# First-wave token lists of two mixture-of-experts layers: added up on the chip instead of read back from DRAM

## The chip, the cores and the metric

One core of a Trainium2 chip runs the whole program. The metric is the device time of one execution in microseconds (us), the median of several runs. Lower is better.

## The reference

Two decoder layers on 1024 tokens of width 1024. Each layer has a mixer and then a mixture of experts; both layers' mixtures have this form:

```python
grp_p, grp_idx = lax.top_k(softmax(xf @ wg_group + bg_group), 1)              # 1 of 4 groups
top_p, top_local = lax.top_k(softmax(in_grp), 2)                              # 2 of its 8 experts
expert_id = grp_idx * EXPERTS_PER_GROUP + top_local
gate = grp_p * top_p / jnp.sum(top_p, axis=-1, keepdims=True)
...
return (jax.nn.silu(xb @ w_gate[e]) * (xb @ w_up[e])) @ w_down[e]             # 1024 -> 256 -> 1024
...
y = jnp.zeros_like(x_tok).at[tok_sorted].add(y_buf[dest] * gate_sorted[:, None])
```

There are 32 experts and 2048 (token, expert) pairs, so an expert gets 64 rows in the mean. Everything is float32.

## The kernel before

The program is a row of blocks. Between two blocks all engines meet: GpSimd (POOL) collects an arrival from each of them and releases them. At some of these places POOL also clears semaphores, with a second meeting behind that; one such place is between the two blocks of this case in the second layer, and none in the first. The blocks of this case occur once in each layer: `project_and_route` (names that begin with `out_`) and `experts` (`ex_`). Rows of the first layer say `even`, those of the second `odd`.

**`project_and_route`** goes through 8 tiles of 128 tokens. In a tile TensorE multiplies by the mixer's output matrix (L1004, each operand split into a high and a low part, so three products stand for one), turns the result (L1025), and multiplies by the router's weights (L1033). VectorE adds the residual (`add_residual`, L871), norms (`norm`, L878), picks the group (`choose_group`, L897 to L905) and the two experts (`choose_experts`, L912 to L922), and finds out where the tile's pairs stand in their experts' lists (`place`, L927 to L935). For that, `count` on TensorE (L1040) multiplies the one-hot choices `both` by a triangle of ones, which gives the number of earlier tokens with the same expert. POOL then writes each pair's token number and result slot into a DRAM table, at row rank * 32 + expert, with two indirect DMAs per tile (L794). The order of work is written out by hand: PE's loop, DVE's loop and POOL's loop each name their steps tile by tile.

After the last tile POOL waits until all 16 table writes have landed, reads the first 128 ranks of all lists back (`Lists.load`, L655), waits for that too, and issues the gathers of the first two experts' rows (`Lists.gather`, L659). VectorE works out the gates and then the low parts of the first expert's weights, which have been loaded in three pieces (two for gate and up, one for down; L987). ScalarE makes the high parts (L852).

**`experts`** works through 32 experts in waves of at most 128 rows each; in this data's executions the first wave is the one that the profile shows. `start` brings up expert 0 and part of expert 1, and `step` then runs once per expert. `turn_x` on TensorE (L1274) turns the gathered rows, ScalarE and VectorE split them (`tokens`, L1348 and L1414), `gate_up` (L1285) makes 12 products for each of the pieces FIRST and SECOND, `gate` and `product` give the hidden values (L1353, L1421), `turn_h` turns them (L1294), and `down` makes 12 products (L1306). Weights of later experts stream in on SP's queue into four buffers, three of which are filled by `project_and_route`; each weight piece is split by ScalarE (`high`, L1338) and VectorE (`low`, L1405) before it is used.

The order at the start of `experts`, and the waits that POOL has at its beginning:

```python
def start(n):            # TensorE
    turn_x(n, 0)
    gate_up(n, 0, FIRST)
    gate_up(n, 0, SECOND)
    turn_x(n, 1)
...
pool.wait_ge(listed, 16 * 2 * NT)
lists.load(pool, 0)
...
def begin():             # POOL, in experts
    pool.wait_ge(zeroed, 1)
    for e in range(2, B):
        gather(0, e)
```

## Time and profile before

| what | us |
|---|---|
| three runs | 2034.01, 2034.46, 2036.6 |
| their median | 2034.46 |
| span of the profiled execution, first to last instruction | 2024.6 |
| what lies around the span (median less span) | 9.9 |
| TensorE busy | 1792.8 (89% of the span) |
| VectorE, ScalarE, POOL busy | 1199.3, 882.3, 312.6 |

The profiled execution's own device time is not listed apart from the three runs; its span is, and the three runs lie within 0.13% of each other. In the profile PE is TensorE's matmuls, PEld its weight loads, DVE VectorE, ACT ScalarE, SP the queue that issues most loads. PEclk is the clock granted to TensorE: 1.00 is 2.4 GHz and 0.50 is 1.2 GHz. A float32 product is shown as two instructions, a product of split (fp32r) or bf16 operands as one. The two places of this case are short against the span: about 31 us in the first layer (846 to 877) and 30 us in the second (1630 to 1660).

### The profile page before, as it was taken

How to read it: one execution, taken by the hardware profiler on the slowest of the kernel's cores; microseconds unless marked ns; L12 is line 12 of the kernel's file. 1: busy time of each engine (PE TensorE's matmuls, PEld its weight loads, DVE VectorE, ACT ScalarE, POOL GpSimd, SP SyncE). 2: the span in 40 equal slices, each digit the busy share in tenths (PEclk: the TensorE clock that was granted, in tenths of full speed). 3: DMA queues.
4: the chain of work that ended last, by engine and by line, in shares of the span. 5: the costliest groups of instructions: out<-in, count | busy, mean ns of one | idle time of the engine just before them, and what ended most of it. 6: DMA issues, size and time to landing. Idle time of an engine off the chain costs nothing. (4 is left out here: it accounts for less than half of the span.)

```text
span 2024.6 us, 25845 instructions
## 1 busy us (share of the span) xinstructions
PE 1792.8 (89%) x9691; PEld 1486.2 (73%) x9691; DVE 1199.3 (59%) x1551; ACT 882.3 (44%) x1060; POOL 312.6 (15%) x254
## 2 busy tenths in 40 slices
PE   8999999577999999759999965999999949999990
PEld 7888889475788888647888744888878837888770
DVE  4323433556655445659999858333235558999884
ACT  4102222362333332338888844111112128888870
POOL 0000000001000001123443310000000123344320
PEclk8999999777999999979999986999999969999995
DMA  5433332802000043559999958111206368999976
GB/s 200 144 120 120 112 130 70 169 1 84 1 1 1 1 153 138 187 220 367 381 373 374 373 205 272 42 52 41 93 4 223 115 243 335 385 381 372 371 282 258
DMA packets 145011, 374.26 MB, mean 185 GB/s; under 512 B 39918, under 2 KB 74862, under 8 KB 120158
## 3 DMA queue, kind: packets, MB, share of 16 engines
q1 hardware_dynamic: 113254, 309.38, 41.6%
q0 software_dynamic: 22432, 45.53, 6.3%
q10 hardware_dynamic: 9216, 17.93, 2.3%
q8 instruction: 64, 1.05, 0.2%
q14 instruction: 45, 0.37, 0.1%
HBM read 331.21 MB, written 75.10 MB: 201 GB/s over the span
## 5 line engine op out<-in xcount | busy, mean ns | idle before, releaser
L1285 PE MATMUL ex_ps_h<-even_split 128*128 128x512 f32 x768 | 194.7, 404 | 7.9 <-DVE even_split L1414 7.6
L1285 PE MATMUL ex_ps_h<-odd_split 128*128 128x512 f32 x768 | 193.1, 402 | 8.0 <-DVE odd_split L1414 7.8
L1285 PEld LDWEIGHTS ex_ps_h<-even_split 128*128 128x128 f32 x768 | 141.7, 191 | 46.8 <-DVE even_split L1414 14.2
L1285 PEld LDWEIGHTS ex_ps_h<-odd_split 128*128 128x128 f32 x768 | 140.3, 189 | 46.8 <-DVE odd_split L1414 14.4
L520 PE MATMUL in_ps<-in_w_hi,in_xT_hi 128*128 128x512 f32 (+1 forms) x448 | 172.5, 385 | 1.7 <-DVE in_xT_lo L425 1.7
L520 PE MATMUL in_ps<-in_w_lo,in_xT_hi 128*128 128x512 f32 (+1 forms) x448 | 169.2, 378 | 0.0
L520 PE MATMUL in_ps<-in_w_hi,in_xT_lo 128*128 128x512 f32 (+1 forms) x448 | 169.2, 378 | 0.0
L1689 PE MATMUL conv_ps<-conv_xT_hi,conv_w_hi 128*128 128x512 f32 x384 | 150.2, 391 | 0.9 <-DVE conv_w_lo L1627 0.9
L1689 PE MATMUL conv_ps<-conv_xT_lo,conv_w_hi 128*128 128x512 f32 x384 | 149.7, 390 | 0.0
L1689 PE MATMUL conv_ps<-conv_xT_hi,conv_w_lo 128*128 128x512 f32 x384 | 149.6, 390 | 0.0
L2410 ACT ACTIVATE att_prob<-att_ps_s 128x512 f32<-128x512 f32 x114 | 67.9, 597 | 154.0 <-PE att_ps_s L2345 153.9
L432 DVE COPY in_stage<-in_ps 128x512 f32<-128x512 f32 (+1 forms) x56 | 36.7, 656 | 161.7 <-PE in_ps L520 161.7
L2359 PE MATMUL att_ps_o<-mix_v,att_prob 128*128 128x128 f32 x912 | 121.4, 278 | 0.4 <-DVE even_attended L2472 0.4
L2359 PEld LDWEIGHTS att_ps_o<-mix_v,att_prob 128*128 128x128 f32 x912 | 117.8, 194 | 4.4 <-ACT att_prob L2410 0.8
L2438 DVE TENSOR_REDUCE att_low<-att_ps_m 128x2 f32<-128x768 f32 (+7 forms) x80 | 71.7, 914 | 49.2 <-PE att_ps_m L2310 47.1
L520 PEld LDWEIGHTS in_ps<-in_w_hi,in_xT_hi 128*128 128x128 f32 x448 | 84.8, 189 | 17.8 <-DVE in_xT_lo L425 2.1
L520 PEld LDWEIGHTS in_ps<-in_w_hi,in_xT_lo 128*128 128x128 f32 x448 | 84.7, 189 | 15.5
L520 PEld LDWEIGHTS in_ps<-in_w_lo,in_xT_hi 128*128 128x128 f32 x448 | 84.9, 190 | 14.4
L1689 PEld LDWEIGHTS conv_ps<-conv_xT_hi,conv_w_hi 128*128 128x128 f32 x384 | 72.4, 188 | 16.1 <-DVE conv_w_lo L1627 1.3
L1004 PE MATMUL out_ps_o<-even_split,even_x_hi 128*128 128x512 f32 x256 | 81.6, 400 | 2.5 <-DVE even_x_lo L939 2.5
L1689 PEld LDWEIGHTS conv_ps<-conv_xT_hi,conv_w_lo 128*128 128x128 f32 x384 | 72.2, 188 | 15.2
L1306 PE MATMUL ex_ps_y<-odd_split,ex_h_hi 128*128 128x512 f32 x256 | 81.8, 401 | 1.6 <-DVE ex_h_lo L1428 1.6
(342 smaller groups left out, 3965.0 us busy)
## 6 DMA issues: line engine op xcount, KB each, us to landing
all_region<-in_moe_w_gate SPq DMA_DIRECT2D x16, 1024.0 KB
all_region<-in_moe_w_up SPq DMA_DIRECT2D x16, 1024.0 KB
all_region<-in_moe_w_down SPq DMA_DIRECT2D x16, 1024.0 KB
experts_w_gu<-in_moe_w_gate SPq DMA_DIRECT2D x16, 1024.0 KB
experts_w_gu<-in_moe_w_up SPq DMA_DIRECT2D x16, 1024.0 KB
experts_w_d<-in_moe_w_down SPq DMA_DIRECT2D x16, 1024.0 KB, 15.2
all_region<-in_ev_w_in SPq DMA_DIRECT2D x12, 1024.0 KB
proj<-in_stage ACTq DMA_DIRECT2D x48, 256.0 KB, 2.1
```

The costliest lines, as they stand in the source:

```text
L432: dve.tensor_copy(stage[:, q % 4, 0:n], ps[:, q % BANKS, 0:n]).then_inc(staged, 1)
L520: last = pe.matmul(ps[:, q % BANKS, 0:n], a[:, k, at], w_part[:, b % 2, k, 0:n], start=(k == 0 and j == 0), stop=(k == KT - 1 and j == 2))
L1004: last = pe.matmul(ps_o[:, t % 2, cols], a[:, k, :], w_part[:, b, k, :], start=(k == 0 and j == 0), stop=(k == KT - 1 and j == 2))
L1285: last = pe.matmul(ps_h[:, u % 2, :], a[:, u % 2, k, :], w[:, k, :], start=(k == 0 and j == 0), stop=(k == KT - 1 and j == 2))
L1306: last = pe.matmul(ps_y[:, at], a[:, u % 2, k, :], w[:, k, at], start=(k == 0 and j == 0), stop=(k == DE // P - 1 and j == 2))
L1689: last = pe.matmul(ps[:, j, at], w_part[:, j, k, :], x_part[:, k, at], start=(k == 0 and q == 0), stop=(k == KT - 1 and q == 2))
L2359: last = pe.matmul(ps_o[:, b, h * P:(h + 1) * P], prob[:, c % 4, h * P:(h + 1) * P], keep.v_all[:, v_at:v_at + P], start=(j == first_tile( ...
L2410: act.activation(prob[:, c % 4, :], ps_s[:, c % 2, :], ACT.Exp).then_inc(exped, 1)
L2438: dve.tensor_reduce(low[:, n % 2, b, hs[0]:hs[-1] + 1], src, X, ALU.max, negate=True).then_inc(reduced, 1)
```

## The change

1. While the tiles go by, the lists of the first 128 ranks are also made on the chip. For each tile and each of the two choices VectorE builds a matrix `placed_at` (tokens by ranks) that holds the token's code at its rank, and TensorE multiplies it by the one-hot choice (`list_places`, two float32 products). VectorE adds each tile's result to `listing` (`take_list`), and `first_lists` turns it into the indices after the last tile. The table is still written, for later waves; the last tile's part is written after the first gathers, and POOL waits for it later, in `experts`.
2. `choose_experts` uses the maximum and index-of-maximum instructions, and `place` two accumulating instructions.
3. `start` of the expert block has a new order on PE, ACT and DVE, and the low part of expert 0's down weights is made in it, no longer in `project_and_route`.
4. SP's first load in `experts` waits for the second gather, POOL in place of DVE clears the row buffers of experts 2 and 3, ScalarE calls Silu once at the end of `project_and_route`, and TensorE makes eight products there whose results nobody reads (`warm_up`).

```diff
     def load(self, pool, w):
         pool.dma_start(self.idx[:], self.table[ds(w * P, P), :, :]).then_inc(self.loaded, 16)
-        pool.wait_ge(self.loaded, w * 16 + 16)
+        pool.wait_ge(self.loaded, w * 16)
...
+        ps_i = ps_c[:, 1, P:P + NE]
...
-                pool.wait_ge(listed, 16 * 2 * NT)
-                lists.load(pool, 0)
+                for t in range(NT - 1):
+                    to_table(t)
                 for s in range(2):
                     pool.wait_ge(xn_stored[s], 16 * (NT // 2))
+
+                pool.wait_ge(lists.ready, 1)
                 for e in range(2):
                     lists.gather(pool, e, data.xg[e], last_token)
+                to_table(NT - 1)
...
+                act.activation(small[:, 5, 0:1], eps[:], ACT.Silu)
...
                 def choose_experts(t):
+                    em_t = em[:, t, :]
+                    dve.drain()
+                    if t >= 2:
+                        dve.wait_ge(some_listed, t - 1)
+                    dve.max(two_of[:, t, :], em_t)
+                    dve.drain()
+                    dve.max_index(e_at[:, t, :], two_of[:, t, :], em_t)
+                    dve.drain()
+                    dve.tensor_copy(e_f[:, t, 0:1], e_at[:, t, 0:1])
...
                 def place(t):
                     dve.wait_ge(counted, t + 1)
                     for c in range(2):
+                        last = dve.scalar_tensor_tensor(v32[:, c, t % 2, :], ps_c[:, 0, 0:NE], 1.0, chosen[:, c, t % 2, :], ALU.mult, ALU.mult,
+                                                        accum_out=rank[:, c, t:t + 1])
+                    last.then_inc(counts_out, 1)
+                    dve.drain()
+                    if t >= 2:
+                        dve.wait_ge(some_listed, t - 1)
+                    for c in range(2):
+                        dve.tensor_scalar(placed_at[:, c, t % 2, :], places[:], rank[:, c, t:t + 1], code[:, c, t:t + 1],
+                                          ALU.is_equal, ALU.mult).then_inc(placed, 1)
...
+                def take_list(t):
+                    dve.wait_ge(some_listed, t + 1)
...
+                        dve.tensor_tensor(listing[:], ps_i, listing[:], ALU.add).then_inc(list_taken, 1)
+                    dve.drain()
+
+                def first_lists():
+
+                    take_list(NT - 1)
+                    dve.tensor_scalar(later_half[:], listing[:], float(S - NOWHERE), -float(S), ALU.is_ge, ALU.mult)
+                    dve.drain()
+                    dve.scalar_tensor_tensor(lists.idx[:, :, 0], listing[:], float(NOWHERE), later_half[:], ALU.add, ALU.add
+                                             ).then_inc(lists.ready, 1)
+                    dve.tensor_scalar(lists.idx[:, :, 1], listing[:], float(NOWHERE), None, ALU.add)
...
-                for piece in range(3):
+                for piece in range(2):
                     hi, lo = data.parts[piece]
...
                 def count(t):
                     pe.wait_ge(picked, t + 1)
                     pe.wait_ge(counts_out, t)
+                    pe.wait_ge(list_taken, t)
...
+                def list_places(t):
+                    pe.wait_ge(placed, 2 * t + 2)
+                    for c in range(2):
+                        last = pe.matmul(ps_i, placed_at[:, c, t % 2, :], chosen[:, c, t % 2, :], start=(c == 0), stop=(c == 1))
+                    last.then_inc(some_listed, 1)
...
                     multiply(t, 1, 0)
+                    if t >= 2:
+                        list_places(t - 2)
                     multiply(t, 1, 1)
...
+                warm_up(pe, ps_o[:, 0, 0:COLS], cst.ident[:], hT[:, (NT - 2) % 2, 0:COLS // P, :].rearrange("p k n -> p (k n)"), 8)
...
                 for u in range(data.lent, B):
+                    if u == data.lent:
+                        sp.wait_ge(gathered[1], 16)
...
                 def begin():
-                    pool.wait_ge(zeroed, 1)
+                    pool.memset(data.later_rows, 0.0)
+                    pool.drain()
                     for e in range(2, B):
                         gather(0, e)
+                    pool.wait_ge(lists.listed, 16 * 2 * NT)
...
                 def start(n):
                     turn_x(n, 0)
                     gate_up(n, 0, FIRST)
+                    turn_x(n, 1)
                     gate_up(n, 0, SECOND)
-                    turn_x(n, 1)
...
                     tokens(n, 0)
                     low(n, 1, FIRST)
+                    tokens(n, 1)
                     product(n, 0)
-                    tokens(n, 1)
+                    low(n, 0, DOWN)
                     low(n, 1, SECOND)
```

The order of instructions at the three places that the prediction speaks of, in the first layer (the second is alike). A row is a source line, an operation, what it writes and reads, its shape, and how often it stands there in a row. `out_ps_c` is the bank of the counts and the lists, `out_hT` the turned rows, `all_region` the first buffer of weights and gathered rows.

TensorE, from the last counts to the first products of `experts`. Before:

```order
L1033 MATMUL out_ps_l<-out_wr,out_hT 128x36 x8
L1040 MATMUL out_ps_c<-out_both,out_before_b 128x32
L1040 MATMUL out_ps_c<-out_both,out_ones_b 128x32 x7
L1071 MATMUL out_ps_c<-out_both,out_ones_b 128x32 x8
L722 UNCONDITIONAL_BRANCH
L1267 UNCONDITIONAL_BRANCH
L1274 MATMUL ex_ps_x<-all_ident,all_region 128x128 x8
L1285 MATMUL ex_ps_h<-even_split 128x512 x24
L1274 MATMUL ex_ps_x<-all_ident,all_region 128x128 x8
```

And with the change:

```order
L1077 MATMUL out_ps_l<-out_wr,out_hT 128x36 x8
L1092 MATMUL out_ps_c<-out_chosen,out_placed_at 128x32 x2
L1085 MATMUL out_ps_c<-out_both,out_before_b 128x32
L1085 MATMUL out_ps_c<-out_both,out_ones_b 128x32 x7
L1092 MATMUL out_ps_c<-out_chosen,out_placed_at 128x32 x2
L1126 MATMUL out_ps_c<-out_both,out_ones_b 128x32 x8
L111 MATMUL out_ps_o<-out_hT,all_ident 128x512 x8
L729 UNCONDITIONAL_BRANCH
L1327 UNCONDITIONAL_BRANCH
L1334 MATMUL ex_ps_x<-all_ident,all_region 128x128 x8
L1345 MATMUL ex_ps_h<-even_split 128x512 x12
L1334 MATMUL ex_ps_x<-all_ident,all_region 128x128 x8
```

The list products (L1092) stand behind the router's and behind the last count, the eight unread products (L111) last in the block, and the second turn now between the two pieces of expert 0.

VectorE, from the last choice to the end of the block. Before:

```order
L922 TENSOR_TENSOR out_both<-out_chosen 128x32
L927 SCALAR_TENSOR_TENSOR out_pos<-out_ps_c,all_iota 128x32
L931 TENSOR_TENSOR out_v<-out_chosen,out_pos 128x32
L933 TENSOR_REDUCE out_dest_f<-out_v 128x1
L931 TENSOR_TENSOR out_v<-out_chosen,out_pos 128x32
L933 TENSOR_REDUCE out_dest_f<-out_v 128x1
L935 CAST out_dest<-out_dest_f 128x2
L969 TENSOR_TENSOR out_t<-out_lg,out_small 128x32
```

And with the change:

```order
L940 TENSOR_SCALAR out_chosen<-all_iota,out_e_f 128x32
L947 SCALAR_TENSOR_TENSOR out_v,out_rank<-out_ps_c,out_chosen 128x32 x2
L954 TENSOR_SCALAR out_placed_at<-out_places,out_rank,out_code 128x128 x2
L956 SCALAR_TENSOR_TENSOR out_dest<-out_rank,out_e_f 128x2
L964 TENSOR_TENSOR out_listing<-out_ps_c,out_listing 128x32
L970 TENSOR_SCALAR out_later_half<-out_listing 128x32
L972 SCALAR_TENSOR_TENSOR even_idx<-out_listing,out_later_half 128x32
L974 TENSOR_SCALAR even_idx<-out_listing 128x32
L1013 TENSOR_TENSOR out_t<-out_lg,out_small 128x32
```

The indices (L972) are now a result of VectorE, five instructions behind the last placing; of the three low parts that follow the gates, two are left.

POOL, from the table writes to the later gathers. Before:

```order
L794 DMA table<-out_codes,out_dest 32768x2 x16
L655 DMA even_idx<-table 128x64
L659 DMA all_region<-xn,even_idx 128x1024 x2
L722 UNCONDITIONAL_BRANCH
L1217 UNCONDITIONAL_BRANCH
```

And with the change:

```order
L807 DMA table<-out_codes,out_dest 32768x2 x14
L659 DMA all_region<-xn,even_idx 128x1024 x2
L807 DMA table<-out_codes,out_dest 32768x2 x2
L729 UNCONDITIONAL_BRANCH
L1275 UNCONDITIONAL_BRANCH
L1190 TENSOR_LOAD all_most
L1190 ISA x2
L1295 MEMSET experts_xg 128x2048
```

The read of the table is gone, and two of its writes stand behind the gathers.

## Rows read from the trace of the kernel before

**Rows 1.** Busy time by stretch: us, PE, PEld, DVE, ACT, POOL, PEclk, DMA share, GB/s.

```profile
728.00:845.50 117.50, 115.73 (x628) 97.86 (x629) 66.89 (x179) 30.65 (x39) 13.28 (x13) 0.99 0.39 137
...
846.00:869.00 23.00, 4.08 (x47) 3.50 (x47) 18.04 (x52) 9.37 (x10) 4.78 (x6) 0.62 0.75 293
```

**Rows 2.** POOL's timeline, first layer: start, length, instruction, idle time before it.

```profile
861.03 0.97 POOL L794 DMA_INDIRECT table<-out_codes,out_dest  x1 [0.30 <-issue]
866.37 0.57 POOL L655 DMA_DIRECT2D even_idx<-table  x1 [4.37 <-DMA table<-out_codes,out_dest]
868.67 1.05 POOL L659 DMA_INDIRECT all_region<-xn,even_idx  x1 [1.73 <-POOLq L722]
```

**Rows 3.** TensorE's timeline: first layer, then second.

```profile
877.58 1.97 PE L1274 MATMUL ex_ps_x<-all_ident,all_region 128*128 128x128 f32 x8 [18.96 <-DMA all_region<-xn,even_idx]
...
1660.14 1.97 PE L1274 MATMUL ex_ps_x<-all_ident,all_region 128*128 128x128 f32 x8 [16.90 <-DMA all_region<-xn,odd_idx]
```

**Rows 4.** Second layer: POOL's first gather, then SP's first load of `experts`.

```profile
1655.80 1.05 POOL L659 DMA_INDIRECT all_region<-xn,odd_idx  x1 [3.64 <-DVEq L78]
...
1659.23 0.33 SPq L635 DMA_DIRECT2D experts_w_gu<-in_moe_w_gate  x1
```

**Rows 5.** VectorE's timeline, first layer: the last choice, its placing, the low parts.

```profile
854.68 0.18 DVE L912 TENSOR_REDUCE out_small<-out_em 128x1 f32<-128x32 f32 x1
...
857.30 0.19 DVE L922 TENSOR_TENSOR out_both<-out_chosen 128x32 bf16<-128x32 f32 x1
857.98 0.19 DVE L927 SCALAR_TENSOR_TENSOR out_pos<-out_ps_c,all_iota 128x32 f32<-128x32 f32 x1 [0.49 <-PE out_ps_c L1040]
...
859.39 0.19 DVE L969 TENSOR_TENSOR out_t<-out_lg,out_small 128x32 f32<-128x32 f32 x1
...
861.06 6.70 DVE L987 TENSOR_TENSOR even_split<-all_region,even_split 128x2048 fp32r<-128x2048 f32 x3
```

**Rows 6.** Single instructions elsewhere: count, min/median/max ns.

```profile
L2035 DVE MATCH_VALUE_LOAD prep_left<-prep_best,prep_imp x16: 81/82/92, 439.0 to 465.1; 128x8 f32 x16
L2035 DVE MATCH_REPLACE8 prep_left<-prep_best,prep_imp x16: 158/159/161, 439.1 to 465.2; 128x16 f32<-128x16 f32 x16
```

**Rows 7.** The same for VectorE's 128x128 TENSOR_SCALAR.

```profile
L2039 DVE TENSOR_SCALAR mix_ext<-prep_left x8: 220/224/229, 439.7 to 465.6; 128x128 f32<-128x128 f32 x8
```

**Rows 8.** TensorE's timeline, first layer: float32 products, the router's and a warm-up.

```profile
809.46 1.87 PE L1033 MATMUL out_ps_l<-out_wr,out_hT 128*128 128x36 f32 x16
...
719.95 5.60 PE L111 MATMUL out_ps_o<-all_ident 128*128 128x128 f32 x48 [1.85 <-PEq L2275]
```

**Rows 9.** TensorE's clock as work resumes, first layer, by stretch.

```profile
884.00:885.00 1.00, 1.00 (x3) 0.78 (x3) 0.00 (x0) 0.00 (x0) 0.00 (x0) 0.50 1.05 434
...
886.00:887.00 1.00, 1.00 (x6) 0.78 (x6) 0.00 (x0) 0.21 (x1) 0.00 (x0) 1.00 0.57 229
```

**Rows 10.** TensorE's timeline, first experts of the first layer.

```profile
881.92 7.52 PE L1285 MATMUL ex_ps_h<-even_split 128*128 128x512 f32 x24 [2.37 <-DVE even_split L1414]
889.28 1.04 PE L1274 MATMUL ex_ps_x<-all_ident,all_region 128*128 128x128 f32 x8
892.88 4.42 PE L1285 MATMUL ex_ps_h<-even_split 128*128 128x512 f32 x12 [2.57 <-DVE even_split L1414]
...
903.72 3.02 PE L1285 MATMUL ex_ps_h<-even_split 128*128 128x512 f32 x12
```

**Rows 11.** The same for the second layer.

```profile
1677.97 3.00 PE L1285 MATMUL ex_ps_h<-odd_split 128*128 128x512 f32 x12
...
1684.42 3.02 PE L1285 MATMUL ex_ps_h<-odd_split 128*128 128x512 f32 x12
```

**Rows 12.** TensorE waiting for a choice in the tile loop, first layer.

```profile
805.66 0.19 PE L1040 MATMUL out_ps_c<-out_both,out_before_b 128*128 128x32 bf16 x1 [0.44 <-DVE out_both L922]
```

**Rows 13.** Where the loads' traffic ends, first layer and second, by stretch.

```profile
860.00:865.00 5.00, 0.00 (x0) 0.00 (x0) 4.66 (x6) 0.01 (x1) 1.70 (x2) 0.50 0.60 248
...
1650.00:1655.00 5.00, 0.00 (x0) 0.00 (x0) 2.39 (x2) 0.00 (x0) 0.58 (x1) 0.50 0.81 336
```

More of the change, by code:

```diff
@@ L696, in project_and_route @@
         v4, t4, e4 = (m.sb(n, [P, NT, NG]) for n in ("v4", "t4", "e4"))
-        em, v32, pos = (m.sb(n, [P, NT, NE]) for n in ("em", "v32", "pos"))
-        chosen = m.sb("chosen", [P, 2, NT, NE])
+        em = m.sb("em", [P, NT, NE])
+        v32 = m.sb("v32", [P, 2, 2, NE])
+        chosen = m.sb("chosen", [P, 2, 2, NE])
         both = m.sb("both", [P, NT, NE], BF16)
         small = m.sb("small", [P, 8, NT])
-        top, gsum, best, second, e2, den, least = (small[:, j, :] for j in range(7))
+        top, gsum, e2, den, least = (small[:, j, :] for j in range(5))
         most_f = m.sb("most_f", [P, 1])
@@ L790, in _, with to_table @@
                 pool.wait_ge(cleared, 16)
-                for t in range(NT):
+                def to_table(t):
                     pool.wait_ge(dest_ready, t + 1)
@@ new lines, in place @@
+                    dve.scalar_tensor_tensor(dest[:, :, t], rank[:, :, t], float(NE), e_f[:, t, :], ALU.mult, ALU.add
+                                             ).then_inc(dest_ready, 1)
+                def take_list(t):
+                    dve.wait_ge(some_listed, t + 1)
+                    if t == 0:
+                        dve.tensor_copy(listing[:], ps_i).then_inc(list_taken, 1)
+                    else:
+                        dve.tensor_tensor(listing[:], ps_i, listing[:], ALU.add).then_inc(list_taken, 1)
+                    dve.drain()
@@ L1067, in _ @@
                 router(NT - 1)
+                list_places(NT - 2)
                 count(NT - 1)
-                pe.wait_ge(counts_out, NT)
+                list_places(NT - 1)
+                pe.wait_ge(list_taken, NT)
                 for t in range(NT):
@@ L1432, in start @@
                     if not isinstance(n, int):
-                        for piece in range(3):
+                        for piece in range(2):
                             low(n, 0, piece)
@@ L1451, in step @@
                         low(*this, DOWN)
-                dve.memset(data.later_rows, 0.0).then_inc(zeroed, 1)
                 rounds(dve, start, step, lambda last: hidden(*last))
```

63 lines of the change are left out of this document (32 added, 31 removed).

## The prediction

> **What bounds the kernel now.** I read the busy time by stretch first. While the tiles go by, TensorE is busy 115.73 of 117.50 us at full clock; between its last product and the experts it works 4.08 of 23.00 us [rows 1]. So a change counts in two ways: what it adds to TensorE inside the tile loop is paid in full, and what it takes from the gap is gained in full. POOL's timeline shows what fills the gap: the last table write starts at 861.03, POOL idles 4.37 us until the writes have landed, the read back costs 0.57 and another 1.73 us, and the first gather starts at 868.67 [rows 2]. TensorE starts at 877.58, released by that gather's data (landing 7.9 us after the gather's end at 869.72), and in the second layer at 1660.14 [rows 3], where the gather ran 1655.80 to 1656.85 (landing 3.3 us later) [rows 4]. VectorE's timeline gives the chain that makes the lists [rows 5].
>
> A difference of 0.2% (4.1 us) is about what a measurement of this kernel tells from none. The sum is made against the span of 2024.6 us and carried over unchanged to the median, 9.9 us above it.
>
> **Part 1: when the first gather can start.** Times are of the first layer; the tail of the second runs the same instructions.
> - Choice of the two experts. Now 9 instructions lead up to `both` in 2.62 us (854.68 to 857.30) [rows 5], 0.29 each. The change has 7: three index or maximum instructions and four of the old kind. No row shows an index-of-maximum; the nearest pair, a value load of 0.08 and a match of 0.16 [rows 6], would give 0.3 with its gap. Two of them, a maximum at 0.25 and four at 0.27 are 2.0 us, 0.6 less. Bounds: at 0.16 each and no gap, 0.9 less; at twice an old instruction (0.58 each), no gain. I take 0.6: `both` at 856.7, and by the row's step of 0.68 to the placing, placing at 857.4.
> - Placing and lists. Two accumulating instructions (0.19 each, plus at most as much for reading the sum: 0.5), a gap of 0.1, two 128x128 at 0.22 [rows 7], two float32 products at the half clock (below, 0.23 each at full: 0.5), a hand-over of 0.1, the addition 0.27, two steps to the indices 0.46. Sum 2.4: indices at 859.8, first gather at 860.1, 8.6 us before today's 868.67. In the second layer the same 2.8 us behind `both` give 1644.7, 11.1 us earlier.
>
> **Part 2: what ends last then.** The experts cannot begin before the meeting between the blocks, and three things now arrive there later than the gather.
> - VectorE. Today it needs 1.67 us from 859.39 to the low parts and 6.70 for three [rows 5]. With two: 859.8 + 0.3 + 1.7 + 4.6 = 866.4.
> - TensorE. Its eight unread products follow the last counts, at 859.7. They are float32 over 512 columns; the nearest row is 24 float32 products over 128 columns in 5.60 us, 0.23 each [rows 8]. Lower bound: time does not grow beyond that of a 512-column instruction of split operands, 0.31 in the mean of 24 [rows 10], two instructions a product: 5 us. Upper: four times the columns, four times 0.23, at half clock all through, 15 us. I take four times at full clock (7.4), plus 1.6 because the clock was at 0.50 from 884 and 1.00 by 886, so some 3 to 4 us of new work pass at half speed [rows 9]: 9.0 us, until 868.7.
> - POOL. Two gathers of 1.0 to 1.1 and two table writes of 0.97 with gaps of 0.3 [rows 2]: until 865.
>
> So TensorE, not the gather, ends the gap in the first layer: with 0.3 for the meeting the experts begin at 869.0 instead of 877.58, 8.6 us earlier. The gather's data is no rival there: it is issued at 860.1, the loads' traffic dies down before 865 [rows 13], and even today's 7.9 us give 869. In the second layer the products run 1644.3 to 1653.3; clearing semaphores costs what today lies between the last gather's end (1658.16) and SP's first load at 1659.23 [rows 4], 1.1 us: 1654.4. The gather's data is due between 1645.8 + 3.3 = 1649.1 and 1645.8 + 7.9 = 1653.7, while the weights' traffic runs until about 1654 (share 0.81 from 1650 to 1655) [rows 13]. I take 1654.5, 5.6 us earlier than 1660.14. Parts 1 and 2 together: 14.2 us.
>
> Here a page of the Trainium skill speaks against the change. Rows of 128 columns cannot show how float32 scales with columns; FP8 and Floating Point Precision, TensorE Precision Notes, says that true FP32 takes four passes through the array. By that rule alone the eight unread products are an estimated 8 x 4 x 0.213 = 6.8 us at 2.4 GHz before any time at half clock, close to the 7.4 that I took from the row; no run here has shown it yet.
>
> **Part 3: the new start.** Count from the first turn, T. Today the third expert's first product comes at T + 26.1 in the first layer (903.72) [rows 10] and T + 24.3 in the second (1684.42) [rows 11]. The first layer pays for the clock: 24 products in 7.52 us where 5.6 would do, a turn of 1.97 instead of 1.04, and 12 products in 4.42 instead of 3.0 [rows 3, 10]. New, with the clock up:
> - turn 1.04, ScalarE's copy 1.02, VectorE's rest 1.23, hand-overs: FIRST at T + 3.4, until 6.2; second turn until 7.2; SECOND until 10.0.
> - ScalarE splits expert 1's FIRST at T + 6.4 to 8.3, its rows to 9.3; VectorE follows with the low part (2.29) to 10.6 and the rows to 11.8. TensorE goes on at T + 11.9.
> - VectorE then has the product (0.6), the moved low part (2.29) and expert 1's SECOND (2.29): until 16.8. TensorE is through with FIRST at 14.7 and waits 2 us. From the start of that SECOND to the third expert's first product it is 6.45 us today (1677.97 to 1684.42) [rows 11]: T + 23.3.
> The start gains 2.8 and 1.0 us, 3.8 together. The moved low part is the reason that it gains no more. Steady steps are unchanged.
>
> **Part 4: what the tile loop pays.** `list_places` stands in it for 6 of 8 tiles, twice: 24 float32 products of 32 columns. The router's 8 of 36 columns take 1.87 us [rows 8], 0.23 each: 5.6 us. Back come waits for `both` such as 0.44 [rows 12], of which the trace has one in each layer: 0.8. Net 4.8 us lost. VectorE has room in this loop, and its new steps replace as many; the new wait of `count` for `list_taken` comes 2.8 us after the residual add, where `both` comes at 2.9 today, so nothing is added. Clearing rows on POOL (1.8 us), Silu's table and SP's wait cost nothing: the rows of experts 2 and 3 are needed 20 us later, ScalarE idles there, and the fourth buffer's weights have 20 us to land. Should the gather come late, SP's wait would cost too.
>
> **Sum.** 14.2 + 3.8 - 4.8 = 13.2 us: span 2011.4, median 2021.3.
>
> **Rivals.**
> 1. *The data is late, or the clock falls in the start.* If the first gather's data must wait until the queued weights are through (rows 13: about 1654.5) and then takes its 3.3 us, the second layer starts at 1657.8, 3.3 us later; today's gather in the first layer, beside loads, took 7.9 instead of 3.3. If the clock falls in each layer's new waits of 2 us, as it fell after an idle of 2.57 us before the row of 4.42, that costs 1.4 each. Together 6.1: 2027. Against it: in the second layer the same idle did not cost the clock.
> 2. *The unread products are short* (5 us). Then VectorE ends the gap: 866.7 in the first layer and about 1652 in the second, if the data is there. 4.8 us more gained: 2016.5.
> 3. *They run at the half clock to the end,* 6 us longer in each layer: 2033, no difference.
> 4. *Slower: the tile loop stalls.* `count` now waits for the previous list to be taken, behind two index-of-maximum instructions. Its margin is 0.1 us. Each 0.1 us beyond it costs TensorE 1.4 us over 14 tiles, so from 0.95 us a tile on the gain is gone: 0.8 instead of 0.3 us for each index-of-maximum. At 1.0 us each the stall is 1.3 us a tile, 18.2 less 13.2: 2039.5. For it: no row shows that instruction. Against it: the match pair takes 0.24 [rows 6].
>
> **Chances.** Forecast 0.62, rival 1 0.15, rival 2 0.14, rival 3 0.05, rival 4 0.04. Faster by over 0.2%: the first three and a little, 0.90; within 0.2%: 0.06; slower: 0.04. The range holds the forecast's bounds, rival 2 and rival 1 with a little more: 2015 to 2029.
>
> **What would show it.** The first gather starts about 3 us after the last `both`, no idle time of POOL before it beyond the wait for VectorE; eight products at L111 of 9 us before the experts; TensorE's first turn some 22 us after the last tile's product instead of 31, at 1.04 us; a wait of 2 us before expert 1's SECOND; list products of 0.47 us a tile. I am wrong if the first turn is still released by the gather's data, or if `count` waits in the tile loop.

## The result and the profile after

The changed kernel takes 2017.44 us in the median of 5 runs (2011.2 to 2019.12), the kernel before 2034.01 in the same session (2028.96 to 2036.6): 0.9927 of it, 95% interval 0.991 to 0.9945. A second set of 6 runs gave 0.9937 (0.9915 to 0.9959). By these ratios that is faster by 14.8 and 12.8 us, with an interval of 8 to 18, where 13.2 were predicted (the first pair of medians lies 16.6 apart). The profiled execution has a span of 2009.6 us and is the shortest of its five runs. A run's time is 1.6 to 1.7 us more than its span wherever both are on record; so of the 9.9 us that the prediction carried over to the median, some 8 tell only that the profiled execution of the kernel before was a short one. They fall out of the difference.

Busy time by stretch of the changed kernel, first layer, answers [rows 1]: the tile loop from its first to its last weight product, the gap up to the experts' first turn, the start up to the third expert's first product.

```profile
722.50:842.05 119.55, 119.11 (x653) 100.64 (x653) 64.88 (x195) 29.80 (x39) 13.50 (x13) 0.99 0.38 135
842.05:865.83 23.78, 16.16 (x73) 9.98 (x72) 16.26 (x61) 10.86 (x12) 7.71 (x6) 0.71 0.79 297
865.83:890.60 24.77, 20.51 (x87) 16.06 (x88) 13.82 (x10) 11.19 (x10) 4.86 (x4) 0.86 0.92 360
```

TensorE was idle for 27.6 of 31.6 us of this gap (845.94 to 877.58 of the kernel before); now it is idle for 7.6 of 23.8. The same six stretches in every trace, cut at the same instructions (us; "rest" is the span without them, code that no kernel here changes):

| kernel | loop, gap, start: layer 1 | layer 2 | sum | rest |
|---|---|---|---|---|
| before | 117.06, 31.64, 26.14 | 109.58, 30.05, 24.28 | 338.8 | 1685.9 |
| changed | 119.55, 23.78, 24.77 | 111.99, 24.79, 24.69 | 329.6 | 1680.0 |
| changed less before | +2.49, -7.86, -1.37 | +2.41, -5.26, +0.41 | -9.2 | -5.8 |

So the total came out near the forecast, but the stretches that the change touches give 9.2 us, not 13.2. The other 5.8 lie in code that is the same in both: the first tile loop began at 722.50 instead of 728.88, 6.4 us earlier, and the later unchanged stretches gave 0.6 back.

TensorE's timeline of the changed kernel, first layer, from the last counts on (start, length, instruction, idle time before it and its releaser); it answers to [rows 3, 10]:

```profile
852.96 0.21 PE L1085 MATMUL out_ps_c<-out_both,out_before_b 128*128 128x32 bf16 x1 [3.10 <-DVE out_both L938]
853.01 0.35 PE L1085 MATMUL out_ps_c<-out_both,out_ones_b 128*128 128x32 bf16 x7
854.46 1.06 PE L1092 MATMUL out_ps_c<-out_chosen,out_placed_at 128*128 128x32 f32 x4 [1.10 <-DVE out_placed_at L954]
855.81 0.40 PE L1126 MATMUL out_ps_c<-out_both,out_ones_b 128*128 128x32 bf16 x8 [0.28 <-DVE out_listing L964]
856.04 9.22 PE L111 MATMUL out_ps_o<-out_hT,all_ident 128*128 128x512 f32 x16
865.83 1.06 PE L1334 MATMUL ex_ps_x<-all_ident,all_region 128*128 128x128 f32 x8 [0.57 <-PEq L729]
869.26 4.43 PE L1345 MATMUL ex_ps_h<-even_split 128*128 128x512 f32 x12 [2.37 <-DVE even_split L1474]
...
879.42 4.31 PE L1345 MATMUL ex_ps_h<-even_split 128*128 128x512 f32 x12 [1.88 <-DVE even_split L1474]
```

The idle time before the first turn is down to 0.57 us and its releaser is TensorE's own queue (the meeting between the blocks), no longer a DMA. The unread products end at 865.26 and the turn runs at full clock (1.06 instead of 1.97). But the first 12 products take 4.43, behind an idle time of 2.37, and expert 1's 4.31: half clock for most of both, where the full clock would give 3.0. The granted clock of the first of them, by stretch:

```profile
869.26:873.69 4.43, 4.43 (x13) 3.43 (x14) 0.00 (x0) 0.00 (x0) 2.30 (x3) 0.64 1.02 431
```

That is 0.64 in the mean, after a turn at full clock (1.00 from 865.83 to 866.89). Cut finer, from the end of the turn on (the idle time, then the products in two parts):

```profile
866.89:869.26 2.37, 0.00 (x0) 0.00 (x0) 1.23 (x1) 1.02 (x1) 1.48 (x1) 1.00 0.72 266
869.26:870.53 1.27, 1.27 (x6) 1.05 (x7) 0.00 (x0) 0.00 (x0) 0.00 (x0) 1.00 1.05 439
870.53:873.69 3.16, 3.16 (x9) 2.38 (x8) 0.00 (x0) 0.00 (x0) 2.30 (x3) 0.50 1.01 428
```

The clock is still at 2.4 GHz through the idle time and the first 1.3 us of the products; only then does it go down to 1.2 GHz. So here it fell after the idle time and not within it; in the second layer it went down at 1648.77, in the last 0.46 us of it.

POOL's timeline, first layer, and VectorE's, which answer to [rows 2, 5]:

```profile
857.99 1.05 POOL L659 DMA_INDIRECT all_region<-xn,even_idx  x1 [6.69 <-DMA xn<-out_xn]
859.34 1.85 POOL L659 DMA_INDIRECT all_region<-xn,even_idx  x1 [0.30 <-issue]
861.50 1.90 POOL L807 DMA_INDIRECT table<-out_codes,out_dest  x1 [0.30 <-issue]
```

```profile
852.65 0.25 DVE L938 SCALAR_TENSOR_TENSOR out_both<-all_iota,out_e_f,out_chosen 128x32 bf16<-128x32 f32 x1
...
853.80 0.60 DVE L954 TENSOR_SCALAR out_placed_at<-out_places,out_rank,out_code 128x128 f32<-128x128 f32 x2
...
856.10 0.19 DVE L972 SCALAR_TENSOR_TENSOR even_idx<-out_listing,out_later_half 128x32 int32<-128x32 f32 x1
...
857.98 4.53 DVE L1031 TENSOR_TENSOR even_split<-all_region,even_split 128x2048 fp32r<-128x2048 f32 x2
```

The indices are there at 856.3, but the gather starts at 857.99: it was released by the store of the last normed rows (`xn`), issued by SP at 847.94, which it has to read. That wait was covered by the read back before. In the second layer VectorE's index is the releaser (below).

The second layer, TensorE:

```profile
1635.61 8.55 PE L111 MATMUL out_ps_o<-out_hT,all_ident 128*128 128x512 f32 x16
1645.79 1.06 PE L1334 MATMUL ex_ps_x<-all_ident,all_region 128*128 128x128 f32 x8 [1.63 <-PEq L78]
1649.23 4.40 PE L1345 MATMUL ex_ps_h<-odd_split 128*128 128x512 f32 x12 [2.37 <-DVE odd_split L1474]
...
1659.38 2.98 PE L1345 MATMUL ex_ps_h<-odd_split 128*128 128x512 f32 x12 [2.11 <-DVE odd_split L1474]
...
1664.01 3.02 PE L1345 MATMUL ex_ps_h<-odd_split 128*128 128x512 f32 x12 [1.43 <-DVE odd_split L1465]
```

### The profile page after: what moved, and what is told of

The parts are those of the page before. It is cut to its first block and busy times, and to the rows that moved or that the text cites. A ratio compares the mean times of both kernels' runs of the same rounds, so it can differ in the third digit from the quotient of the medians.

```text
span 2009.6 us, 26040 instructions
## 1 busy us (share of the span) xinstructions
PE 1814.2 (90%) x9786; PEld 1498.5 (75%) x9787; DVE 1194.1 (59%) x1603; ACT 883.8 (44%) x1062; POOL 321.3 (16%) x260
## 3 DMA queue, kind: packets, MB, share of 16 engines
q8 instruction: 64, 1.05, 0.2%
## 5 line engine op out<-in xcount | busy, mean ns | idle before, releaser
L1345 PEld LDWEIGHTS ex_ps_h<-even_split 128*128 128x128 f32 x768 | 141.0, 190 | 46.8 <-DVE even_split L1474 13.6
L1749 PEld LDWEIGHTS conv_ps<-conv_xT_lo,conv_w_hi 128*128 128x128 f32 x384 | 72.4, 189 | 14.9
```

The source lines that it names most:

```text
L1345: last = pe.matmul(ps_h[:, u % 2, :], a[:, u % 2, k, :], w[:, k, :], start=(k == 0 and j == 0), stop=(k == KT - 1 and j == 2))
L1749: last = pe.matmul(ps[:, j, at], w_part[:, j, k, :], x_part[:, k, at], start=(k == 0 and q == 0), stop=(k == KT - 1 and q == 2))
```

## The experiments

Each gives its median and its ratio to the kernel before; the reasons rest on the six stretches, which tell a microsecond where the times do not.

**What ends the gap: the products left out.**

```diff
-                warm_up(pe, ps_o[:, 0, 0:COLS], cst.ident[:], hT[...], 8)
```

> The changed kernel without its 8 unread float32 products; nothing else. Yardsticks of the changed kernel (first layer / second): the gap from the last product of the tile loop to the experts' first turn 23.78 / 24.79 us, the start from that turn to the third expert's first product 24.77 / 24.69. Theory A (the products end the gap in the first layer by 0.6 us, POOL's last table write in the second): the gap shrinks by 0.6 and 0 us, and without work before them the first turn (1.06) runs at half clock (about 2) and the first 12 products stay at 4.4; sum about 1 us slower. Rival B (the products alone hold the experts up, POOL is no limit): the gap shrinks by 2.7 us in each layer, down to VectorE's end at 862.5 (and 2.1 in the second): 4 to 5 us faster. Rival C (the products keep the clock up and so carry the start): the start grows by more than 1.5 us in each layer, 3 us slower or more.

Measured 2022.15 us, 0.9947 (0.9929 to 0.9965). Gaps 21.47 and 24.49 against 23.78 and 24.79, starts 26.66 and 26.79 against 24.77 and 24.69. Its TensorE, in the first layer and in the second:

```profile
871.01 1.94 PE L1333 MATMUL ex_ps_x<-all_ident,all_region 128*128 128x128 f32 x8 [6.81 <-PEq L729]
875.32 5.49 PE L1344 MATMUL ex_ps_h<-even_split 128*128 128x512 f32 x12 [2.37 <-DVE even_split L1473]
...
1652.35 1.97 PE L1333 MATMUL ex_ps_x<-all_ident,all_region 128*128 128x128 f32 x8 [9.79 <-DMA all_region<-xn,odd_idx]
```

In the first layer the gap shrank by 2.3 us: rival B is right there, the products ended it and VectorE is next (its low parts end at 870.48 here, the turn starts 0.53 later). POOL was no limit at all: its last table write runs from 871.66 to 872.65, past the first turn. In the second layer only 0.3 is to be had, since the gather's data comes next. And rival C is right as well: without the products the turn and the first 12 run at half clock throughout, and the start grows by 1.9 and 2.1. The eight products give back 1.4 us more than they cost.

**Fewer products, table writes first.**

```diff
-                for t in range(NT - 1):
+                for t in range(NT):
                     to_table(t)
...
                     lists.gather(pool, e, data.xg[e], last_token)
-                to_table(NT - 1)
...
-                warm_up(..., 8)
+                warm_up(..., 4)
```

> The changed kernel with the last tile's two table writes ahead of the first gathers, where POOL idles 6.7 us, and 4 unread products instead of 8. Theory A (TensorE and POOL end the gap within 0.6 us of each other, VectorE 2.7 us before): POOL is through by about 861, TensorE by 860.5, VectorE ends the gap at 862.5 of the first layer; the gap shrinks by 2.5 us in each layer if the gathered rows are there, 4 to 5 us faster in all. Rival B (the gather's data is the next limit): it was issued at 858.0 and lands 3.3 to 7.9 us later, so the gap shrinks by 0 to 2.5 us, and the first turn is then released by the gather. Rival C (fewer products, clock down): the gap shrinks, but the start grows by 1.5 us in each layer: 1 to 2 us faster.

Measured 2015.45 us, 0.993 (0.9909 to 0.9951). Gaps 21.67 and 24.68, starts 25.88 and 26.68. In the first layer the gap shrinks by 2.1 us, nearly as in theory A, down to VectorE (its low parts end at 870.23, the turn starts 0.53 later). In the second it shrinks by 0.1 and the gather's data releases the turn, as rival B has it. Rival C holds in both: the starts grow by 1.1 and 2.0. POOL's first gather and TensorE's first turn in the second layer:

```profile
1642.79 1.03 POOL L659 DMA_INDIRECT all_region<-xn,odd_idx  x1 [0.30 <-issue]
```

```profile
1651.68 1.97 PE L1333 MATMUL ex_ps_x<-all_ident,all_region 128*128 128x128 f32 x8 [4.94 <-DMA all_region<-xn,odd_idx]
```

The data lands 7.86 us after the gather's end (1643.82 to 1651.68); in the kernel without products it was 7.84 (1644.51 to 1652.35). The same 7.9 from the gather's end at 1637.72 of the changed kernel give 1645.6, against its turn at 1645.79: in the second layer the data is there at about the time when the meeting behind the unread products (1644.16) is over, so it is the next bound at once. The sum of the six stretches, 330.7, is no better than with eight products; the clock took what the gap gave.

**The old order of the start, in the changed kernel.**

```diff
                     gate_up(n, 0, FIRST)
-                    turn_x(n, 1)
                     gate_up(n, 0, SECOND)
+                    turn_x(n, 1)
```

The same on ScalarE and VectorE, and three low parts ahead of the experts.

> The changed kernel with the old order of the start on TensorE, ScalarE and VectorE, and three low parts before the experts again (the third DOWN). Theory A (the new order gained nothing here: with the clock falling in the 2.4 us after the first turn either order takes 24.5 us): start 24 to 25 us in both layers, the gap grows by 0 to 0.3 us as VectorE ends at 864.8 and TensorE at 865.3: no difference in time, within 1 us. Rival B (the new order is worth the 3.8 us of the prediction, and the clock took it back): start 26 to 27 us in both layers, 3 to 4 us slower.

Measured 2021.7 us, 0.9954 (0.9939 to 0.9969). Starts 25.24 and 25.05, gaps 23.79 and 24.82. Theory A: the order, with the moved low part, is worth 0.5 and 0.4 us, not the prediction's 2.8 and 1.0. In both orders the clock fell behind the first turn (4.40 and 4.61 us for the first 12 products here); what the new order is worth with the clock held up has not been measured. (Its median is 3 to 4 us above the changed kernel's; its six stretches show 0.3 to 1.2, and the third low part costs the gap nothing.)

**The new order alone, in the kernel before.** The same lines the other way round.

> The kernel before with the new order of the start alone (TensorE, ScalarE, VectorE, third low part moved behind the first product). Theory A (the order is worth little: it saves the second turn's place in the queue but puts a low part of 2.29 us ahead of the second expert's): start 25 to 26.5 us in the first layer, against 26.14, and 25.5 to 27 in the second, against 24.28, with a half clock there; gap of the first layer unchanged, since it waits for the gather's data: no gain, up to 2 us slower. Rival B (it is worth the 3.8 us of the prediction): 23.3 us in the second layer, 24 in the first.

Measured 2032.28 us, 1.0009 (0.9994 to 1.0024). Starts 26.48 and 25.88 against 26.14 and 24.28: no gain by itself, as theory A has it.

**The moved low part, behind instead of ahead.**

```diff
                     product(n, 0)
-                    low(n, 0, DOWN)
                     low(n, 1, SECOND)
+                    low(n, 0, DOWN)
```

> The changed kernel with VectorE's low part DOWN of the first expert behind, not before, SECOND of the second expert. Theory A (this part of 2.29 us makes the wait of 1.43 us before expert 1's SECOND in the second layer; in the first, where products at half clock hide it, it costs nothing): the wait is gone, the start of the second layer 23.3 us instead of 24.69, the first 24.8 as before: 1.4 us faster, too little for the times, plain in the trace. Rival B (DOWN is then late for the first down products): a wait appears before them, and the start of the next step grows by up to 2 us.

Measured 2016.22 us, 0.9929 (0.991 to 0.9948). Starts 24.56 and 23.05 against 24.77 and 24.69: the wait of 1.43 us in the second layer is gone, and no new one stands ahead of the down products. Theory A.

**A bridge over the idle time behind the first turn**, on top of it:

```diff
                 def start(n):
                     turn_x(n, 0)
+                    if isinstance(n, int):
+                        warm_up(pe, ps_y[:, 0:P], ident[:], ident[:], 10)
```

> The changed kernel with VectorE's DOWN behind SECOND, and 10 unread float32 products of 128 columns (0.23 us each) on TensorE between the first turn and the first expert's products, where it idles 2.4 us. Theory A (the clock falls in that idle time and costs 1.4 us on expert 0's first 12 products, 4.4 instead of 3.0, and more behind them): those 12 take 3.0 us, ScalarE's split of expert 1 starts 1.4 earlier, the start is 21.5 to 22.5 us in both layers against 24.56 and 23.05 without the bridge: 2 to 4 us faster than that kernel. Rival B (the clock falls anyway, in the wait of 2 us before expert 1): the first 12 take 3.0, but expert 1's 4.4; the start falls by 0.5 to 1.4 us. Rival C (the clock of the start follows the half speed of earlier work, not that idle): nothing changes.

Measured 2016.96 us, 0.9922 (0.99 to 0.9945). Starts 21.58 and 21.60 against 24.56 and 23.05. TensorE, first layer:

```profile
875.48 1.06 PE L1334 MATMUL ex_ps_x<-all_ident,all_region 128*128 128x128 f32 x8 [0.57 <-PEq L729]
876.38 2.40 PE L111 MATMUL ex_ps_y<-all_ident 128*128 128x128 f32 x20
878.91 3.02 PE L1345 MATMUL ex_ps_h<-even_split 128*128 128x512 f32 x12
881.78 1.03 PE L1334 MATMUL ex_ps_x<-all_ident,all_region 128*128 128x128 f32 x8
882.57 2.98 PE L1345 MATMUL ex_ps_h<-even_split 128*128 128x512 f32 x12
887.66 2.98 PE L1345 MATMUL ex_ps_h<-even_split 128*128 128x512 f32 x12 [2.12 <-DVE even_split L1476]
```

The 12 products are back at 3.02 us, and the clock did not fall behind the wait of 2.12 ahead of expert 1's either (2.98). Theory A: 4.4 us less in the two starts. The median does not show them. In the trace 2.7 of them went elsewhere in the second layer: its tile loop took 113.28 us instead of 111.80, with a wait of 0.97 for `out_h` at its first turn, and its gap 26.07 instead of 24.81, where the unread products took 9.75 us (8.73 in the kernel without the bridge). The sum is 325.8 against 327.6, and the rest was 1689.5.

**Five unread products, one bridge; then two bridges.** The second kernel has 8 more products of 128 columns behind `gate_up(n, 0, SECOND)`.

> As the kernel with bridge and DOWN behind SECOND, but with 5 unread products instead of 8 before the experts. In the first layer VectorE ends at 0.5 us before the experts' first turn as the traces with 4 and with none show (gap 21.67 and 21.47 us against 23.78 with 8), in the second the gather's data (24.68 and 24.49 against 24.79). Theory A: gap 21.6 and 24.7, and the bridge keeps the start at 22 us: 2 us faster than with 8. Rival B (with 4 or none the clock was down in the start: 25.88 and 26.68, 26.66 and 26.79 us): five are not enough to carry it over the idle time before the turn, the start grows by 1 to 2 us in each layer, and the time is no better than with 8.

Measured 2014.95 us, 0.9913 (0.9893 to 0.9933). Gaps 21.40 and 24.61, starts 23.26 and 23.19; expert 1's first 12 products take 4.40 and 4.57. Both: the gap is won as theory A has it, and most of it is lost again in the start, as B has it.

> As the kernel with 5 unread products, the bridge and DOWN behind SECOND, and 8 more unread products of 128 columns between the first expert's last product and the second expert's first, where TensorE idles 2.1 us. Theory A (it was that second idle time, after only five unread products, that let the clock fall and made expert 1's first 12 products 4.4 and 4.6 us): they take 3.0, gaps stay at 21.4 and 24.6, starts fall from 23.26 and 23.19 to 21.7 us: about 3 us faster than with one bridge, some 8 us faster than the changed kernel, 2009 to 2011. Rival B (the clock falls for what went before): the 12 products stay at 4.4 us and nothing is gained.

Measured 2015.96 us, 0.992 (0.9906 to 0.9934). Its TensorE, first layer:

```profile
880.32 2.99 PE L1345 MATMUL ex_ps_h<-even_split 128*128 128x512 f32 x12
883.14 1.95 PE L111 MATMUL ex_ps_y<-all_ident 128*128 128x128 f32 x16
885.45 2.99 PE L1345 MATMUL ex_ps_h<-even_split 128*128 128x512 f32 x12 [0.35 <-DVE even_split L1478]
```

Theory A for the clock: 2.99 instead of 4.40. The six stretches come to 322.4 us (119.54, 21.52, 21.63; 112.56, 24.62, 22.57), 7 to 8 less than the changed kernel's and the least of all. (In the second layer the first turn itself ran at half clock, 1.97 us: the five products had ended 4.1 us before it.) The runs do not confirm that: 2009 to 2011 were expected, and the median lies 1.5 us below the changed kernel's first and 3.1 below its second, with intervals that overlap. The trace had a rest of 1692.3 us, the second highest of fourteen. That this version beats the changed kernel is shown for the stretches, not for the time.

**The list products twice.**

```diff
-                    for c in range(2):
+                    for c in (0, 1, 0, 1):
                         last = pe.matmul(ps_i, placed_at[:, c, t % 2, :], ...)
```

> The changed kernel with the products of list_places issued twice (the same result). It prices the list products in the tile loop. Theory A (TensorE pays each of them in full: 0.36 us from a list product's start to the next weight product's, for 6 tiles): each tile loop grows by 2.2 us, to 121.7 and 114.2, and the gap by up to 1.4, as the last two tiles' lists stand in it at half clock, 0.7 us each. Rival B (0.47 a tile, two products at 0.23, as predicted): 2.8 us in each loop. Rival C (they lie beside waits): under 1 us.

Measured 2027.72 us, 0.9986 (0.9972 to 1.0). The first tile loop is 122.27 us, 2.72 more, the gaps 24.62 and 26.73. A pair more costs the tile 0.45: rival B, near the 0.47 of the prediction. The second loop, 116.19, is 4.2 longer, but 1.37 of it is a wait for `out_h` at the loop's first turn, which the first trace of the changed kernel does not have; 2.8 remain. The six stretches come to 339.7 us, 9 to 10 more than the changed kernel's, and its median is 8.7 and 10.3 us above the changed kernel's two: here the stretches and the times agree.

**Both kernels again**, to see what varies.

> The kernel before once more, unchanged, to see which stretches of it vary. The stretches that the change touches (tile loops 117.06 and 109.58, gaps 31.64 and 30.05, starts 26.14 and 24.28 us) differ by 9.2 us between the two kernels' traces, but the runs by 15 to 16. Theory A (the rest is chance of the two profiled executions: until its first product of the tile loop the kernel before took 728.88 us in a fast one of its runs, and the changed kernel 722.50 to 729.97 in five traces): these six stretches come back within 0.3 us each, and the time before them is longer, 730 to 736. Rival B (the six stretches vary from run to run): one of them is longer by a microsecond or more, in the first layer's gap or start above all. Rival C: nothing differs, and the medians differ for a reason that no stretch shows.

> The kernel before a third time, unchanged. The stretches that the change touches were 338.8 and 339.9 us in two traces, against 329.6 in the changed kernel's: 9.2 to 10.4 us; the medians differ by 15. Theory A (the rest is chance in code that the change does not touch, which took 1683.0 to 1693.8 us in three traces of the kernel before and its like and 1680.0 to 1688.6 in five of the changed one and its like): the six stretches sum to 338.5 to 340.5 again. Rival B (in its usual runs the first gather's data lands later than in these two): the gap of the first layer is 33 us or more.

> The changed kernel a second time. Theory A: tile loops 119.5 and 112, gaps 23.8 and 24.8, starts 24.7 and 24.7 us, each within 0.3, sum 329 to 330.5; the time before the first product of the tile loop anywhere from 722 to 732. Rival B: one of the six differs by over a microsecond from the first trace, and the sum of 329.6 was luck.

Measured 2029.76 (0.9999, 0.9985 to 1.0012) and 2030.38 us (0.9995, 0.9983 to 1.0008) for the kernel before, 2019.02 for the changed one.

| trace | time before the first tile loop | six stretches | sum | rest |
|---|---|---|---|---|
| before, again | 722.26 | 117.25, 32.10, 26.68; 109.26, 30.24, 24.40 | 339.9 | 1683.0 |
| before, third | 727.85 | 117.09, 31.75, 26.00; 109.62, 30.18, 25.81 | 340.5 | 1688.1 |
| changed, again | 726.75 | 119.56, 23.79, 24.79; 112.71, 24.84, 24.78 | 330.5 | 1688.1 |

The sums hold: 338.8 to 340.5 against 329.6 and 330.5, 9.7 us in the mean. The rest does not: 1683.0 to 1693.8 in four traces of the kernel before and its like, 1680.0 to 1692.3 in ten of the changed one and its like, with means of 1687.7 and 1687.5. So the 5.8 us of the first pair of traces can be put down to chance: before the first tile loop alone the kernel before had 722.26 the second time, the changed one 726.75. The times say a little more than the stretches, though. All 77 runs of the kernel before have a mean of 2031.2 us and the 11 of the changed one 2017.7: 13.5 apart, with a standard error of 1.4, against 9.7. And the kernel with the list products twice has the six stretches of the kernel before (339.7), yet its runs are 2.8 us faster (interval 0 to 5.7). Some 3 to 4 us of the gain are seen in the times and found in no stretch of these traces. The one start that varied is the second layer's of the kernel before, 24.28, 24.40 and 25.81; in the last TensorE's clock fell behind a wait that had left it up in the other two:

```profile
1677.07 4.31 PE L1285 MATMUL ex_ps_h<-odd_split 128*128 128x512 f32 x12 [2.56 <-DVE odd_split L1414]
```

## Why the prediction was right, and where it was not

- **What bounds the kernel** held: additions to the tile loop were paid in full (+2.49 and +2.41), and what left the gap was gained (7.86 and 5.26).
- **Part 1, choice of the experts**: the steps up to `both` take 1.99 us (850.66 to 852.65) instead of 2.62, 0.63 less, predicted 0.6; `both` starts 10.6 us behind the last weight product of the loop (842.05) instead of 11.4 (845.94), and 11.2 instead of 11.8 in the second layer. An index-of-maximum is a value load of 0.09 and a search of 0.185; with its gap 0.33, where 0.3 was put. Rival 4 was without ground.
- **Part 1, placing and lists**: from the start of the placing (853.39) to the indices 2.9 us against 2.4; the two 128x128 instructions took 0.60 and the list products, at half clock, 1.06. Then the gather came 1.7 us after the indices in the first layer and 0.8 in the second (hand-over put at 0.3), 15.9 and 15.7 us behind the last weight product instead of 14.2 and 14.6. Two things failed. The hand-over to POOL was put too low: it took 0.83 us in the second layer, in this trace and in the eight others with this order of POOL's steps. And in the first layer a wait on the store of `xn`, hidden before, was not looked for. Neither cost anything here, since in both layers the products and the meeting end the gap; but in the second layer the gather's data is the next bound, and what makes it late there is the hand-over and the longer placing, not the store. So two of the signs that the prediction named did not come: the gather 3 us behind the last `both` (it was 5.3), and POOL idle for nothing but VectorE.
- **Part 2**: VectorE was forecast to be done 20.5 us behind the last weight product, and was, to the tenth (862.51 less 842.05). The products took 9.22 and 8.55 us for 9.0. The weight loads of the changed kernel show the working:

```profile
858.74 0.34 PEld L111 LDWEIGHTS out_ps_o<-out_hT,all_ident 128*128 128x128 f32 x1 [0.52 <-issue]
859.60 0.34 PEld L111 LDWEIGHTS out_ps_o<-out_hT,all_ident 128*128 128x128 f32 x1 [0.52 <-issue]
...
863.38 0.19 PEld L111 LDWEIGHTS out_ps_o<-out_hT,all_ident 128*128 128x128 f32 x1 [0.24 <-issue]
863.81 0.19 PEld L111 LDWEIGHTS out_ps_o<-out_hT,all_ident 128*128 128x128 f32 x1 [0.24 <-issue]
```

  Two instructions a product, 0.85 apart at the half clock (granted 0.50 until 860) and 0.43 at the full: 0.86 a product, 6.9 us for eight, and some 2.3 on top, as the first 4 us passed at half speed. The prediction had 7.4 and 1.6; the two errors cancelled. By the Trainium skill's FP8 and Floating Point Precision, TensorE Precision Notes, four passes make an estimated 6.8 at full clock: the trace agrees with its 6.9. Rivals 2 and 3 fell. The meeting took 0.57 and 1.63 us instead of 0.3 and 1.1. Gain 13.1 us against 14.2.
- **POOL** was forecast to be through 19 us behind the last weight product and was at 22.6 (864.69), since it began later and its second gather and first table write took 1.85 and 1.90 us beside VectorE's low parts. Nothing waits for it, as the kernel without the products shows.
- **Part 3 failed.** The start was to take 23.3 us in both layers and took 24.77 and 24.69: a gain of 1.0 in place of 3.8 (1.37, and -0.41). The step that was wrong is "with the clock up": the forecast had FIRST from T + 3.4 until 6.2, it ran until 7.9, since the clock fell behind the 2.37 us of idle time ahead of it; with unread products in that time it did not (`bridge_down`, 3.02). Rows 10 showed such a fall after 2.57 us; in the sum I took it for the mark of a cold start. ScalarE splits expert 1 only when FIRST is through, so the loss moved down the chain: expert 1 began at T + 13.6, not 11.9. With the bridge it began at T + 12.2, and with DOWN behind SECOND the start took 21.6. The moved low part is the reason for 1.4 us of it in the second layer, at the place named; in the first it hid behind slow products. Rival 1 had this clock loss in the wait ahead of expert 1, 1.4 us a layer. There it came in the first layer (4.31 us behind a wait of 1.88) and not in the second (2.98 behind 2.11); behind the first turn, where the rival did not look, it came in both. The rival's other half, data 3.3 us late, did not come: so half of its mechanism was true, and mostly at another place.
- **Part 4** held in its size: 2.49 and 2.41, together 4.9 for 4.8. But `count` waits for the list once a layer, 0.30 and 0.41 us:

```profile
800.31 0.18 PE L1085 MATMUL out_ps_c<-out_both,out_before_b 128*128 128x32 bf16 x1 [0.30 <-DVE out_listing L964]
```

  The prediction had named a wait of `count` as a sign that it is wrong, and on this point it was: its sum had no wait left in the loop. The wait stands in the place of the one for `both`, 0.44 and 0.37 before [rows 12], and is no longer than it, so it is no stall as in rival 4. With the waits taken out a pair costs 0.44 and 0.40 us a tile, not 0.47. The two errors nearly cancel.
- **Sum**: 13.1 + 1.0 - 4.9 = 9.2 us by the traces against 13.2. The measured 12.8 and 14.8 are nearer to the forecast than its own steps deserve, and that is luck: the start gave 2.8 us less than forecast and the gap 1.1 less, and the times have about as much more that no stretch shows. 9.7, the difference of the mean sums, lies within the second interval (8 to 17 us) and just outside the first (11 to 18), and nearly three standard errors below the 13.5 of all runs. Chance in the unchanged code explains the first pair of traces, but what the remaining 3 to 4 us are stays open.

## What to carry to other kernels

Work put on TensorE only to keep its clock has to reach up to the products it is meant for: eight unread products before a turn did not save the twelve behind it, as 2.4 us of waiting lay between, and ten short ones in that wait did. When a wait is removed, list what else the waiting instruction reads and when that lands (here the store of `xn`, and the gathered rows 7.9 us behind their gather): these can be the next bounds. And compare the stretches that a change touches over several traces before crediting it with the difference of two spans; here 5.8 of 15.0 us was the rest of the program varying.

## What the runs showed of the hardware

- Idle times of nearly one length had either outcome for TensorE's clock. It fell behind 2.37 us ahead of the first products in both layers of the changed kernel, after eight unread products and a turn at full clock. Ahead of expert 1 of the same kernel it fell behind a wait of 1.88 in the first layer (4.31 for 12 products) and held through 2.11 in the second (2.98). With eight and the bridge it held through 2.12 and 2.11; with five and the bridge it fell behind 2.15 and 2.08 (4.40 and 4.57). In the second layer of the kernel before it held through 2.56 in two traces (2.99 for the next 12 products) and fell behind 2.56 in the third (4.31).
- In the kernel before, the first gather's data releases the turn 3.2 to 3.4 us after the gather's end in the second layer, where most of the weights are through [rows 3, 4] (DMA share 0.36 from 1655 to 1660), and 7.8 to 7.9 in the first, where SP's loads are issued beside it (four traces). In the second layer of the changed kernel and its like, where weights are still under way, it comes after 7.3 to 7.9 us.
- POOL's indirect DMAs take 1.0 us alone and 1.85 to 3.03 when they begin within one of VectorE's low parts (128x2048). The second gather of the second layer, beside a low part that ran from 1637.55 to 1639.85:

```profile
1636.69 1.03 POOL L659 DMA_INDIRECT all_region<-xn,odd_idx  x1 [6.46 <-DVE odd_idx L972]
1638.03 2.69 POOL L659 DMA_INDIRECT all_region<-xn,odd_idx  x1 [0.31 <-issue]
```

  It ended 0.88 us behind the low part's end, and so did all others: in the gaps of the ten traces with the lists made on the chip, each one that began more than 0.1 us into a low part ended 0.87 to 0.92 us behind the end of that part, however early it had begun, while those that began before or with one took 0.97 to 1.05. The Trainium skill, SBUF — State Buffer, Terms, tells of a port pair that VectorE and GpSimd share by an exclusive lock, held for the whole instruction; this agrees with it, and no run here isolates it.
